# One TensorE matmul per token tile of the bias in place of a VectorE addition, in the decay projection of a hybrid attention and recurrence block

## What is computed

```python
def rwkv7_mixer(r, k, v, w_lo, a_lo, g_lo, w0, w2, a0, a2, g2, k_k, k_a, r_k, gn_g, gn_b):
    w = -jax.nn.softplus(-(w0 + jnp.tanh(w_lo) @ w2)) - 0.5
    decay = jnp.exp(-jnp.exp(w.astype(f32)))
    a = jax.nn.sigmoid(a0 + a_lo @ a2)
    ...
```

## Time and profile before

| | |
|---|---|
| median of 3 executions | 2844.08 us |
| lowest and highest | 2842.68 and 2846.38 us |
| profiled execution | 2842.68 us |
| its span in the trace | 2840.8 us |
| TensorE, VectorE, ScalarE, GpSimd busy | 94%, 62%, 34%, 3% of the span |
| granted TensorE clock, mean | 0.976 of 2.4 GHz |

### The profile page before, as it was taken

One profiled execution on the slowest core, in us unless ns is written; L12 is line 12 of the kernel. 1 busy time (PEld: TensorE's weight loads), 2 busy tenths in 40 slices (PEclk: granted clock), 3 DMA queues, 4 the chain that ended last, 5 costly groups with the idle time before them and its releaser, 6 DMA issues. The chain is left out here.

```text
span 2840.8 us, 47378 instructions
## 1 busy us (share of the span) xinstructions
PE 2683.6 (94%) x19368; PEld 2214.9 (78%) x19368; DVE 1756.1 (62%) x2869; ACT 968.1 (34%) x1731; POOL 88.0 (3%) x121
## 2 busy tenths in 40 slices
PE   6999999999799999699999998899997999999998
PEld 5888887887577778588888886687775888887887
DVE  5866665767444472277777775753444856666666
ACT  4332222113333433244444444442432323222122
POOL 0000000000000000111111110000000000000000
PEclk9999999999899999799999999999998999999999
DMA  4222223224423385611111110530031222223224
GB/s 138 82 85 74 74 85 107 104 103 153 102 86 97 107 271 140 164 43 40 40 35 29 36 40 26 212 127 1 30 119 56 82 89 85 74 73 119 103 89 156
DMA packets 230632, 260.91 MB, mean 92 GB/s; under 512 B 63426, under 2 KB 186560, under 8 KB 230464
## 3 DMA queue, kind: packets, MB, share of 16 engines
q1 hardware_dynamic: 228880, 256.91, 28.3%
q10 hardware_dynamic: 1584, 1.60, 0.2%
HBM read 189.17 MB, written 64.06 MB: 89 GB/s over the span
## 5 line engine op out<-in xcount | busy, mean ns | idle before, releaser
L715 PE MATMUL f_ps<-hi,f_wh 128*128 128x512 f32 x768 | 302.1, 393 | 19.3 <-DVE f_wl L501 11.9
L717 PE MATMUL f_ps<-hi,f_wl 128*128 128x512 f32 x768 | 300.8, 392 | 0.0
L715 PE MATMUL f_ps<-f_t1h,f_wh 128*128 128x512 f32 x480 | 187.1, 390 | 0.0
L716 PE MATMUL f_ps<-f_t1l,f_wh 128*128 128x512 f32 x480 | 186.8, 389 | 0.0
L715 PEld LDWEIGHTS f_ps<-hi,f_wh 128*128 128x128 f32 x768 | 145.5, 189 | 52.4 <-issue 10.7
L2051 PE MATMUL fr_dense_ps<-hi,fr_wh 128*128 128x512 f32 x400 | 167.0, 417 | 7.1 <-DVE fr_wl L2342 7.1
L717 PEld LDWEIGHTS f_ps<-hi,f_wl 128*128 128x128 f32 x768 | 145.5, 189 | 30.4
L715 PE MATMUL f_ps<-f_t2h,f_t3h 128*128 128x512 f32 x384 | 151.6, 395 | 7.8 <-DVE one_y L607 3.7
L2052 PE MATMUL fr_dense_ps<-one_lo,fr_wh 128*128 128x512 f32 x400 | 156.8, 392 | 0.0
L2053 PE MATMUL fr_dense_ps<-hi,fr_wl 128*128 128x512 f32 x400 | 156.8, 392 | 0.0
L716 PE MATMUL f_ps<-f_t2l,f_t3h 128*128 128x512 f32 x384 | 150.9, 393 | 0.0
(11 more groups left out here) (419 smaller groups left out, 6458.8 us busy)
## 6 DMA issues: line engine op xcount, KB each, us to landing
one_y<-in_w_in SPq DMA_DIRECT2D x25, 512.0 KB, 4.4
f_raw<-in_ffn_w_gate SPq DMA_DIRECT2D x11, 1024.0 KB, 5.4
f_raw<-in_ffn_w_up SPq DMA_DIRECT2D x11, 1024.0 KB, 7.9
act<-one_y SPq DMA_DIRECT2D x44, 256.0 KB, 2.1
f_raw<-in_ffn_w_down SPq DMA_DIRECT2D x11, 1024.0 KB, 4.9
f_raw<-act SPq DMA_DIRECT2D x11, 1024.0 KB, 4.8
early<-in_ffn_w_gate SPq DMA_DIRECT2D x11, 1024.0 KB, 5.4
early<-in_ffn_w_up SPq DMA_DIRECT2D x11, 1024.0 KB, 7.9
```

The lines of the kernel that those rows point to most:

```text
L715: nc.tensor.matmul(out, wh, xh, start=start, stop=False)
L716: nc.tensor.matmul(out, wh, xl, start=False, stop=False)
L717: return nc.tensor.matmul(out, wl, xh, start=False, stop=stop)
```

## The change

The addition of `w0` moves from VectorE to TensorE. For each of the 8 token tiles of a step, the product runs over the 64 rows that hold data (`lora[0:64]`, `w2[0:64]`), and a second matmul over one row (`ones` x `w0`) is accumulated onto it in PSUM. `w2_full`, its memset and the semaphores `w2_zeroed` and `raised` go. `w0` is loaded as one row of 512 and not broadcast over 128 partitions; a row of 128 ones is loaded in one more DMA (13 for 12 in the count of small loads). The sigmoid waits for the product itself. In the planner `zadd` goes, `zw` is given 3.8 for 3.6, and the lateness of `load_mem` is 5 for 16. The last line keeps the `ones_row` input as a two-dimensional array.

```diff
--- before.py
+++ after.py
@@ -1717,9 +1717,8 @@
     for p in range(PAIRS):
         q = p and p - 1
         k, r, v = (at[(n, p)] for n in "krv")
-        event(("zw", p), "pe", 3.6, ("tanh",), room(("zw", p)))
-        event(("zadd", p), "dve", 1.4, ("zw", p))
-        event(("sg", p), "act", 2.3, ("zadd", p), p and ("cum", q, 1))
+        event(("zw", p), "pe", 3.8, ("tanh",), room(("zw", p)))
+        event(("sg", p), "act", 2.3, ("zw", p), p and ("cum", q, 1))
         for h in range(2):
             event(("cum", p, h), "pe", 1.9, ("sg", p), room(("cum", p, h)))
             event(("dec", p, h), "act", 2.0 + 1.2 * (h == 0), ("cum", p, h), p and ("res", q), p and ("store_ops", q))
@@ -1747,7 +1746,7 @@
         event(("tcopy", n), "act", 1.2 if n < PAIRS + 2 else 0.4, ("turn", n), n and ("tcopy", n - 1), 2 <= n < PAIRS + 2 and ("store_v", n - 2))
         if n < PAIRS + 2:
             event(("store_v", n), "sp", 0.2, ("tcopy", n), late=4.0)
-    event(("load_mem",), "sp", 0.5, ("store_ops", 3), ("store_bonus", 3), late=16.0)
+    event(("load_mem",), "sp", 0.5, ("store_ops", 3), ("store_bonus", 3), late=5.0)
     for t in range(2):
         event(("msq", t), "act", 1.9, ("load_mem",), t and ("msq", 0))
         event(("mxn", t), "dve", 1.5, ("msq", t), t and ("mxn", 0))
@@ -1794,7 +1793,7 @@
     at = {kind: c for c, kind in enumerate(KINDS)}
     DH, G, NB, HID, ST = 64, 2, 63, 256, 16
     NC = G * NB
-    SMALL = 16 * 12
+    SMALL = 16 * 13
     with core.stage() as ctx:
         raw = y[:, 0:2, :].rearrange("p a (k n) -> p a k n", n=P)
         krv = y[:, 2:8, :].rearrange("p (a n) t -> p a n t", n=3)
@@ -1806,7 +1805,6 @@
         xr = sbuf(nc, ctx, f"{tag}_xr", [P, 3, T])
         vt = sbuf(nc, ctx, f"{tag}_vt", [P, 2, TT, P])
         w2 = sbuf(nc, ctx, f"{tag}_w2", [P, RW])
-        w2_full = sbuf(nc, ctx, f"{tag}_w2_full", [P, RW])
         g2 = sbuf(nc, ctx, f"{tag}_g2", [P, RW])
         vecs = sbuf(nc, ctx, f"{tag}_vecs", [P, 6, PAIRS])
         mu = sbuf(nc, ctx, f"{tag}_mu", [P, 2, MIXED])
@@ -1827,7 +1825,7 @@
         rate, sq, u, sg, g_of, g_gain = (six[:, n, :] for n in range(6))
         xs, r_hi, r_lo = six[:, 0:2, :], six[:, 2:4, :], six[:, 4:6, :]
         cos, sin = dec[:, 0, :], dec[:, 1, :]
-        w0 = xr[:, 2, 0:RW]
+        w0, ones = xr[0:1, 2, 0:RW], xr[0:1, 2, RW:RW + P]
         tri, pairsum = xr[:, 2, RW + P:RW + 3 * P], xr[:, 2, RW + 3 * P:T]
         lora, glo = lg[:, 0, :], lg[:, 1, :]
         c_kv = krv[:, 0, 0:2, :]
@@ -1846,7 +1844,6 @@
         vec_step, hi_split, lo_split, multiplied, evacuated, mixed = (
             s(n) for n in ("vec_step", "hi_split", "lo_split", "multiplied", "evacuated", "mixed"))
         wide_mm, wide_read, squashed = s("wide_mm"), s("wide_read"), s("squashed")
-        w2_zeroed, raised = s("w2_zeroed"), s("raised")
         rate_mm, rate_done, squared, norm_mm, rooted = (s(n) for n in ("rate_mm", "rate_done", "squared", "norm_mm", "rooted"))
         g_mm, g_copied, g_read, sum_mm, bonus_read, bonus_done = (
             s(n) for n in ("g_mm", "g_copied", "g_read", "sum_mm", "bonus_read", "bonus_done"))
@@ -1907,12 +1904,13 @@
                     lead(sp, c - (CHUNKS - 8))
 
             def load_small():
-                sp.dma_start(w2_full[0:64, :], a["rwkv_w2"]).then_inc(small_in, 16)
+                sp.dma_start(w2[0:64, :], a["rwkv_w2"]).then_inc(small_in, 16)
                 sp.dma_start(w2[64:P, :], a["rwkv_a2"]).then_inc(small_in, 16)
                 sp.dma_start(g2[:], a["rwkv_g2"]).then_inc(small_in, 16)
-                sp.dma_start(w0, a["rwkv_w0"].rearrange("(o n) -> o n", o=1).broadcast_to([P, RW])).then_inc(small_in, 16)
+                sp.dma_start(w0, a["rwkv_w0"].rearrange("(o n) -> o n", o=1)).then_inc(small_in, 16)
                 sp.dma_start(tri, a["tri_decay"]).then_inc(small_in, 16)
                 sp.dma_start(pairsum, a["pairsum"]).then_inc(small_in, 16)
+                sp.dma_start(ones, a["ones_row"]).then_inc(small_in, 16)
                 with nc.allow_non_contiguous_dma("vectors per channel"):
                     for n, v in enumerate(("a0", "k_k", "k_a", "r_k", "gn_g", "gn_b")):
                         sp.dma_start(vecs[:, n, :], a[f"rwkv_{v}"].rearrange("(c p) -> p c", p=P)).then_inc(small_in, 16)
@@ -2032,10 +2030,6 @@
                 sp.wait_ge(v_stored[b], 48)
                 sp.wait_ge(rot_stored[b], 96)
 
-        @block.gpsimd
-        def _(pool):
-            nc.gpsimd.memset(w2_full[64:P, :], 0.0).then_inc(w2_zeroed, 1)
-
         @block.tensor
         def _(pe):
             def mm_half(c, h):
@@ -2104,10 +2098,10 @@
                     chan = of_tile(p)
                     pe.wait_ge(small_in, SMALL + 16)
                     pe.wait_ge(squashed, 1)
-                    pe.wait_ge(w2_zeroed, 1)
                     wide_free(e)
                     for t in range(TT):
-                        mm = nc.tensor.matmul(wide_ps[:, of_tile(t)], lora[:, of_tile(t)], w2_full[:, chan], start=True, stop=True)
+                        nc.tensor.matmul(wide_ps[:, of_tile(t)], lora[0:64, of_tile(t)], w2[0:64, chan], start=True, stop=False)
+                        mm = nc.tensor.matmul(wide_ps[:, of_tile(t)], ones, w0[:, chan], start=False, stop=True)
                     mm.then_inc(wide_mm, 1)
                 elif e[0] == "cum":
                     wide_free(e)
@@ -2253,7 +2247,7 @@
                     nc.scalar.activation(glo, glo, ACT.Sigmoid).then_inc(squashed, 1)
                 elif e[0] == "sg":
                     p = e[1]
-                    act.wait_ge(raised, p + 1)
+                    act.wait_ge(wide_mm, use_of(("zw", p)) + 1)
                     nc.scalar.activation(sg, wide_ps[:], ACT.Sigmoid).then_inc(wide_read, 1)
                 elif e[0] == "dec":
                     p, h = e[1], e[2]
@@ -2330,13 +2324,7 @@
                 dve.wait_ge(vec_step, 3)
 
             for e in plan:
-                if e[0] == "zadd":
-                    p = e[1]
-                    dve.wait_ge(small_in, SMALL + 16)
-                    dve.wait_ge(wide_mm, use_of(("zw", p)) + 1)
-                    tiles = wide_ps[:].rearrange("p (t c) -> p t c", c=P)
-                    nc.vector.tensor_tensor(tiles, tiles, w0[:, of_tile(p)].unsqueeze(1).broadcast_to([P, TT, P]), ALU.add).then_inc(raised, 1)
-                elif e[0] == "w_lo":
+                if e[0] == "w_lo":
                     c = e[1]
                     dve.wait_ge(hi_split, c + 1)
                     nc.vector.tensor_tensor(w_lo[:, c % 2], raw[:, c % 2], w_hi[:, c % 2].bitcast(F32), ALU.subtract).then_inc(lo_split, 1)
@@ -2485,6 +2473,7 @@
         "pairsum": same.astype(f),
         "mean_pair": same.astype(f) / f(CH),
         "mean_all": np.full((P, P), 1.0 / RW, f),
+        "ones_row": np.ones((1, P), f),
         "eye": (s == t).astype(f),
         "m_gram": np.stack([s < t, s <= t], 1).astype(f),
         "m_low": (s > t).astype(f),
@@ -2994,7 +2983,7 @@
 
 def block_kernel(nc, a, out):
 
-    f = {n: (v[0] if len(v.shape) > 1 and v.shape[0] == 1 else v) for n, v in a.items()}
+    f = {n: (v[0] if len(v.shape) > 1 and v.shape[0] == 1 and n not in ("ones_row",) else v) for n, v in a.items()}
 
     def scratch(name, shape):
         return nc.dram_tensor(name, shape, F32, kind="Internal").ap()
```

## The result

The changed kernel takes 2884.45 us (median of 4 runs, 2882.50 to 2889.45) against 2843.68 us for the kernel before (4 runs on the same chip): 1.0139 times as long, 95% interval 1.0127 to 1.0151, or +40.8 us. The forecast was 2864.5 us, range 2851 to 2870.5. So the direction was right, but the cost is about twice what I gave it and outside the range.

What follows compares the result with a forecast made beforehand. TensorE was taken to bound the changed stage up to 1030 us. Steps +20.1, addition 0, loads and memset 0, planner +0.9 sum to +21.0 us: 2863.7, by the median 2865.1, forecast 2864.5 us, range 2851 to 2870.5.

Steps and rivals of the forecast that it cites:

- What bounds the stage: Projection and preparation, 758 to 1030 us: TensorE busy 271.18 of 272 us, so its time is on the path, VectorE's not.
- 32 records and 17 changes of shape, +20.1 us: Each of four changed steps: 32 records at 0.112 us plus 17 shape changes at 0.19, 6.81 us a step.
- Rival A: Changed steps: one row after 64 is no change of shape; +9.6 us, about 2853; chance 0.27.
- Rival C: Changed steps: the one-row matmul runs beside the 64-row one, so not slower; +1.6 us, 2845.7; chance 0.04.
- rival D: Stage's end: earlier memory work clears two TensorE waits, -4.6 instead of +0.9; faster, at best 2841 us; chance 0.02.
- The addition, the loads, the memset at 0: Changed stage: removed VectorE addition (4 x 1.225 us), extra DMA (about 0.43 us) and removed GpSimd memset all count 0.
- The planner, +0.9: Stage's end: memory square goes ahead of rotation split 0, stalling TensorE 5.5 us for the silu; +0.9 left after absorption.
- The waits of 1.03 and 3.56: TensorE's waits at 1043.47 (gather) and 1059.91 (second silu), claimed to absorb 1.0 and 3.6 us of the planner's stall.
- rival B: Planner's stall isn't absorbed, or the clock falls behind the steps (6 us); +25.6 in all, 2869.7; chance 0.10.

Runs made afterwards that it cites:

- the two runs: The changed kernel with the memory load's lateness back at 16: 2880.97 us; the kernel before with that lateness alone set to 5: 2846.74 us.

## Why the prediction was right, and where it failed

**What bounds the stage: right.** TensorE is busy for all of 758 to 1030 in the changed kernel and for 271.18 of 272 us before, and what was put on it there arrived at the end: in most runs to within 3 us of what the steps and the dense matmuls behind them took more, in the first run with 64 and 64 rows with 5 us on top that stay open.

**32 records and 17 changes of shape, +20.1 us: right.** The change's first seven matmuls are 0.41 us apart. The run with 64 and 128 rows gives the price with the clock at 1.00: from the last dense matmul before a step to the second behind it are 771.23 - 764.11 = 7.12 us, where the run with 128 and 128 rows takes 4.03, so 16 changes cost 3.09, 0.19 each. With a seventeenth a step takes 7.31; the kernel before takes 2.24 so measured, so the four steps cost 20.3 more. Rival A (64 to 1 is no change) falls by the 0.41 us. Rival C (overlap) falls too: no one-row matmul is hidden; rival D with it, as nothing is faster. (C's 2845.7 left out the +0.9 of the planner, and its limit, (5.7 - 0.9) / 4, is 1.2 us and not 1.1; neither changes anything.) The Trainium skill's rule (TensorEngine Tiling (Array Packing), Tiling Modes), that a change of the tiling mode drains the engine, agrees with the 0.19 us paid for 64 with 1, 64 with 128, 128 with 1, and, where the clock still holds, 64 with 32 rows.

**The addition, the loads, the memset at 0: right** as far as they were tried: the first by the run with the bias folded in (+0.3 us, within the interval). The loads weren't tried by themselves.

**The planner, +0.9: mechanism right, mis-sized.** The square went ahead of the split, the silu came late, TensorE waited 7.32 us for 1.10, 6.2 more where I said 5.5. The waits of 1.03 and 3.56 went, as forecast. What the sum lacked is the clock behind the long wait (0.61 from 1065 to 1078): from the reader of the silu to the next product of the compression TensorE takes 1085.72 - 1071.09 = 14.63 us, before 1043.47 - 1030.29 - 1.03 = 12.15, so it cost 2.5. 6.2 + 2.5 - 4.6 = 4.1, against +3.9 to the second compression output and +4.3 to the transposes in the traces, and about 3 by the two runs.

**The step that failed is the clock: the sum has no term for it.** The forecast took the clock to stay at 1.00 through the steps and behind them, and left a fall to rival B. I wrote that "the stretch 1400 to 1420 is full of such groups at a granted clock of 1.00", gave B 0.10 in all, and priced a fall at 6 us behind the steps alone. Those groups are broken up as the changed steps are, but each of them keeps 64 rows in a tile, and their loads are spaced 0.029 us a record, so several tiles of the array are at work. The changed step has a one-row matmul in every second place. I took the interruptions for what the clock might react to, and looked for a row that had them; what the runs show it to react to is how few rows the matmuls use, and for that no row of the kernel before could speak. I knew that no row showed a one-row matmul, and asked it only about the change of shape.

The size, by the trace: the four steps take 35.5 us, 8.9 more than at full clock (26.6: the 26.0 of the run with 64 and 128 rows, and 0.17 a step for the last change, which it lacks), and the dense matmuls behind them 7.6 more than those of the kernel before. That is 16.5 us where the forecast has 0 and rival B 6. The sum in its place: 20.3 for the changes and records + 16.5 for the clock = 36.8 of the 36.9 to the first compression product, + 4.3 for the end of the stage, - 2.3 at its start, - 3.5 after it: 35.3 of the 35.6.

**The Trainium skill on the weight load** (TensorE: Matmul & The Clock Gate, Part 3): its statement that a load overlaps a matmul in flight only where the row group differs disagrees with one more shape: with 64 rows in both matmuls, all in the same row group, the records start 0.112 us apart (a step of 32 takes 3.76 us, 3.58 of them records) with loads of 188 ns each, so these are hidden.

No kernel tried beats the kernel before; the one with the bias folded into a spare row equals it (1.0003, 0.9994 to 1.0012).

## What to carry to other kernels

Where TensorE is the bound, a bias belongs in a spare row of a matmul that runs anyway, or on an engine with slack, not in a one-row matmul of its own: here that paid for its columns in full, for each change of shape (0.19 us), and with the clock of what follows. An operation taken off an engine that isn't the bound is worth nothing until a wait of the bounding engine is shown to end with it. When a new instruction has a shape that no row shows, ask every question of it, the clock's too, and give what can't be answered a price and a chance.

## What the runs showed of the hardware

- TensorE's granted clock fell from 1.00 to 0.5 (2.4 to 1.2 GHz) while the engine issued without idle time, where every second matmul used 1 or 32 rows (0.51 from 766 to 776 in the change), and also where 2 us of one-row matmuls stood in one block ahead of 64-row ones (0.57 from 767 to 771). In the profiled executions it did not fall where the matmuls used 64 or 128 rows, with 16 changes of shape a step, nor with zeros in 127 of 128 rows of the loaded operand (1.00 from 758 to 1030).
- It was low, too, while and after TensorE waited 7.32 us for the silu (0.61 from 1065 to 1078), and the dense matmuls behind that wait were 0.43 us apart where 0.23 is full speed.
- A change between shapes by rows costs 0.19 us of TensorE for 64 with 1, 64 with 128, 128 with 1 and 64 with 32 rows: the spacing is 0.41 us a matmul of two records where 0.22 would do.
- Beside 64-row matmuls a matmul of one row costs as much as one of 128 for the same columns (0.41 us with either), and its weight load takes 184 ns.
